# Summing a mixture of experts' outputs on the chip by 0/1 matmuls, in place of a scatter to DRAM and a read back

## The reference, cut to what matters

```python
g_sel = jnp.argmax(lc, axis=-1)
lf_sel = jnp.take_along_axis(lf, g_sel[:, None, None], axis=1)[:, 0]
top_v, top_i = lax.top_k(lf_sel, TOP_K_FINE)
top_w = jax.nn.softmax(top_v, axis=-1)
gates = p_sel * one_hot(g_sel) * fine
h = jax.nn.silu(hg) * hu * gates
y = y + jnp.einsum('tef,efd->td', h, w_down[e])
...
x = x + hier_moe(rmsnorm(x, g2), ...)
return rmsnorm(x, final_norm_g)
```

## Time and profile before

| | |
|---|---|
| median of 3 runs | 735.38 us (735.12 to 735.39) |
| span of the profiled execution | 733.9 us |
| which of the runs was profiled | not given; the median lies 1.5 us above its span |
| TensorE busy | 594.7 us (81%) |
| VectorE / ScalarE / GpSimd busy | 24% / 15% / 12% |
| moved by DMA | 238.7 MB, of them 9.46 MB by gathers and scatters |
| expert stage, first gate/up to end of the last down product | 224.4 to 702.8 us |

### The profile page before, as it was taken

The page is one execution under the profiler, slowest core; times in us unless marked ns, Lnnn a source line. Parts: engine busy times, 40 slices in busy tenths (PEclk is TensorE's granted clock), DMA queues, the critical chain, the costliest instruction groups (busy, mean ns, idle before and its releaser), DMA issues.

```text
span 733.9 us, 8110 instructions
## 1 busy us (share of the span) xinstructions
PE 594.7 (81%) x3112; PEld 316.7 (43%) x3112; DVE 176.2 (24%) x322; ACT 107.1 (15%) x202; POOL 88.0 (12%) x146
## 2 busy tenths in 40 slices
PE   7999999999888999999776776778777777777820
PEld 5999999878753333333222222222222222222200
DVE  5554248514456010101000001000000100000037
ACT  6422342203210000000000000000000000000013
POOL 1000000000022212121121111111211111110000
PEclk9999999999979999999999999999999999999975
DMA  9930600286189999999999999999999999999756
GB/s 290 346 98 3 229 1 1 81 340 269 58 330 342 399 415 415 416 417 415 417 415 416 417 416 417 418 415 416 416 417 416 417 416 415 417 417 418 274 148 227
DMA packets 57128, 238.71 MB, mean 325 GB/s; under 512 B 9382, under 2 KB 16567, under 8 KB 40723
## 3 DMA queue, kind: packets, MB, share of 16 engines
q1 hardware_dynamic: 51987, 228.96, 78.9%
q0 software_dynamic: 5120, 9.46, 3.5%
HBM read 232.48 MB, written 13.24 MB: 335 GB/s over the span
## 4 chain that ended last, share of the span: by engine, by line
SPq 51%; PE 34%; DMA 6%; DVE 4%; issue 3%; ACT 1%; POOLq 0%; POOL 0%; DVEq 0%
SPq L458 33%; SPq L465 18%; PE ps L1283 12%; PE ps L1354 7%; PE ps L1445 5%; DMA w<-in_moe_w_up 3%; PE ps L1465 2%; PE ps L1380 1%; DMA y_rows<-ybuf,idc_y 1%; PE ps L1247 1%; PE ps L1249 1%; PE ps L1248 1%; DMA gain<-in_norm_g 1%; DVE yfin L826 1%; DVE x_sb L826 1%
## 5 line engine op out<-in xcount | busy, mean ns | idle before, releaser
L1445 PE MATMUL ps<-w,xT 128*64 128x512 f32 x1024 | 231.1, 596 | 57.5 <-DMA w<-in_moe_w_up 57.5
L1445 PEld LDWEIGHTS ps<-w,xT 128*64 128x64 f32 x1024 | 72.7, 137 | 214.1 <-issue 151.3
L1465 PE MATMUL ps<-wd,hexT 128*64 128x512 f32 x512 | 118.6, 604 | 27.7 <-DVE hexT L1164 27.7
L820 DVE TENSOR_TENSOR hexp<-silu_g,ps 128x256 f32<-128x256 f32 x32 | 13.5, 422 | 419.7 <-ACT silu_g L795 419.7
L594 POOL DMA_INDIRECT y_rows<-ybuf,idc_y x32 | 32.9, 1029 | 380.0 <-ACT ybuf L799 380.0
L1465 PEld LDWEIGHTS ps<-wd,hexT 128*64 128x64 f32 x512 | 38.1, 138 | 87.4 <-issue 52.8
L795 ACT ACTIVATE silu_g<-ps 128x256 f32<-128x256 f32 x32 | 12.3, 384 | 279.3 <-PE ps L1445 279.3
L1283 PE MATMUL ps<-hT_hi,wi_hi 128*128 128x288 f32 x224 | 48.7, 299 | 0.0
L1283 PE MATMUL ps<-hT_lo,wi_hi 128*128 128x288 f32 x224 | 48.0, 296 | 0.0
L799 ACT COPY ybuf<-ps 128x512 f32<-128x512 f32 x32 | 18.8, 586 | 179.6 <-PE ps L1465 179.6
L582 POOL DMA_INDIRECT xg<-hn_rows,idc_x x32 | 33.8, 1055 | 27.5 <-POOL idc_x L579 27.5
(11 more groups left out here) (194 smaller groups left out, 507.0 us busy)
## 6 DMA issues: line engine op xcount, KB each, us to landing
w<-in_moe_w_gate SPq DMA_DIRECT2D x64, 1024.0 KB, 18.9
w<-in_moe_w_up SPq DMA_DIRECT2D x64, 1024.0 KB, 23.7
wd<-in_moe_w_down SPq DMA_DIRECT2D x64, 1024.0 KB, 22.2
wo<-in_w_out SPq DMA_DIRECT2D x2, 2048.0 KB, 11.0
yfin<-y_rows SPq DMA_DIRECT2D x8, 512.0 KB, 6.0
x_sb<-in_x_prompt SPq DMA_DIRECT2D x4, 512.0 KB, 8.6
hn_rows<-hn2p SPq DMA_DIRECT2D x4, 512.0 KB, 3.0
out<-yfin SPq DMA_DIRECT2D x4, 512.0 KB, 2.6
```

The costliest lines, as they stand in the source:

```text
L1445: last = mm(ps[64 * h:64 * h + 64, 1, :], lhs, w1[s][:, :, k, h * (F // 2):(h + 1) * (F // 2)], start=(k == 0), stop=(k == KD - 1))
L1465: last = mm(ps[64 * h:64 * h + 64, 3, :], lhs, wd[s][:, c, h * 512:(h + 1) * 512], start=(c == 0), stop=(c == F // P - 1))
```

## The change

The scatter, the DRAM tensor `y_rows`, the read back and `yfin` are gone. Each block's down product is scaled by its gate on ScalarE into `y_hi` (rounded to float32r), and VectorE writes the rest of it into `y_lo`. VectorE also builds `home`, a tile of 0 and 1 with one column for each of the 576 tokens: 1 where the block's row belongs to that token and half. TensorE multiplies `home` with `y_hi` and `y_lo` for each of the five token tiles (`send_home`): four one-pass matmuls of 512 columns, two on partitions 0 to 63 into one PSUM bank and two on 64 to 127 into another. VectorE adds the two banks to `x_sb` (`add`, two instructions of 512 columns). The five tiles of block n - 1 are done within block n: three of them inside gate/up, one behind `transpose_x`, one behind `transpose_act`. A pair of banks is free again once the add two tiles back is done.

The routing makes a second table, the gate of each row (`gate_of`), by 20 more small matmuls for the first blocks and 20 for the further ones. All 32 blocks are written out; the check for further blocks stands between blocks 29 and 30 (`LAST` = 30), with all homes and adds of block 29 ahead of it, and block 30 has no homes of an earlier block. The index copies on GpSimd are gone for the 32 blocks.

```diff
-            def scatter(col, s, n, done, i):
-                if not (isinstance(i, int) and i == 0):
-                    pool.wait_ge(y_out[s], 16 * i)
-                nc.gpsimd.tensor_copy(idc_y[:, s:s + 1], idx[:, 1, bass.ds(col, 1)]).then_inc(idc_ready, 1)
-                pool.wait_ge(idc_ready, done)
-                pool.wait_ge(y_ready, n + 1)
-                pool.sem_inc(idc_seen, 1)
-                nc.gpsimd.indirect_dma_start(
-                    out=y_rows, out_offset=bass.IndirectOffsetOnAxis(ap=idc_y[:, s:s + 1], axis=0),
-                    in_=ybuf[:, s, :], in_offset=None,
-                    bounds_check=4 * T - 1, oob_is_err=False).then_inc(y_out[s], 16)
...
+            def high(S, n, done, buf, gate):
+                act.wait_ge(S["dn_ps"], done)
+                nc.scalar.activation(y_hi[:, buf, :], ps[:, 3, :], ACT.Copy, scale=gate).then_inc(S["hi_ready"], 1)
...
+            def low(S, n, buf, row, gate):
+                ts(home[:, buf, :], row_ids[:], row, None, ALU.is_equal)
+                dve.wait_ge(S["hi_ready"], n + 1)
+                stt(y_lo[:, buf, :], ps[:, 3, :], gate, y_hi[:, buf, :].bitcast(F32), ALU.mult,
+                    ALU.subtract).then_inc(S["lo_ready"], 1)
+
+            def add(S, n, j, turn, seen):
+                m = TOK[j]
+                dve.wait_ge(S["home_ps"], seen)
+                for h in range(2):
+                    c = slice(h * (D // 2), (h + 1) * (D // 2))
+                    last = tt(x_sb[0:m, j, c], ps[0:m, 4 + 2 * (turn % 2) + h, :], x_sb[0:m, j, c], ALU.add)
+                last.then_inc(S["added"], 1)
...
+            def turn(n, adds, more=True):
+                if adds:
+                    for j in range(3):
+                        add_first(n - 1, j)
+                work_h(main, n)
                 if more:
-                    work(n + 1)
-                work_hT(n)
...
+                    work(main, n + 1)
+                if adds:
+                    add_first(n - 1, 3)
+                work_hT(main, n)
+                if adds:
+                    add_first(n - 1, 4)
...
+            def send_home(S, buf, j, turn):
+
+                n, t = TOK[j], slice(j * P, j * P + TOK[j])
+                for part, y in enumerate((y_hi, y_lo)):
+                    for h in range(2):
+                        r = slice(64 * h, 64 * h + 64)
+                        last = mm(ps[0:n, 4 + 2 * (turn % 2) + h, :], home[r, buf, t], y[r, buf, :], start=(part == 0),
+                                  stop=(part == 1))
+                last.then_inc(S["home_ps"], 1)
...
+            def turn(n, homes, more=True):
+                s, need = n % NSLOT, 32 * (n // NSLOT + 1)
+
+                def between(k):
+                    if homes and k in (1, 3, 5):
+                        home_first(n - 1, k // 2)
+
+                gate_up(main, n, s, w1_in[s], need, between)
+                if more:
+                    transpose_x(main, (n + 1) % NSLOT, xg_in[(n + 1) % NSLOT], 16 * ((n + 1) // NSLOT + 1))
+                if homes:
+                    home_first(n - 1, 3)
+                transpose_act(main, n)
+                if homes:
+                    home_first(n - 1, 4)
```

More of the change, by code:

```diff
@@ L65 @@
 NSLOT = 3
-PRE = [(NE - s + NSLOT - 1) // NSLOT for s in range(NSLOT)]
-ROUNDS = NE // NSLOT
+SPARE = 2
+LAST = NE - NSLOT + 1
 OUTSIDE = 4096
@@ L236, in build @@
     hexT = post("hexT", [P, 2, P])
+    routing_at = where["end"]
     t_g = post("t_g", [P, NT, NG])
@@ L254, in build @@
     t_k = post("t_k", [P, NT * 2, MAX_J])
+    back = region(routing_at, where["zp"])
+    y_hi = back("y_hi", [P, 2, D // 2], F32R)
+    y_lo = back("y_lo", [P, 2, D // 2], F32R)
+    home = back("home", [P, 2, T], F32R)
     p1 = region(where["zp"], pool_end)
@@ L371, in build, with blocks_past @@
     segs = ((0, 0, HT, 0, 0), (1, 0, SEQ - HT, HT, 0), (1, SEQ - HT, HT, SEQ, 1))
[L375 to L384, removed]
+    def blocks_past(eng, before, body, after):
         eng.wait_ge(nov_ready, 1)
@@ L388, in blocks_past, with nothing @@
         with eng.If(count > 0):
+            before()
             with eng.Fori(0, count) as b:
                 body(b)
-        return count
+            after(count)
+    def nothing(*_):
+        return None
     with nc.Block() as block:
@@ L509, in _ @@
-            with sp.Fori(1, ROUNDS) as i:
-                for s in range(NSLOT):
-                    refill(i, s)
-            for n in range(NSLOT * ROUNDS, NE):
-                refill(n // NSLOT, n % NSLOT)
+            for n in range(NSLOT, NE):
+                s, done = n % NSLOT, n - NSLOT + 1
+                sp.wait_ge(main["half_ps"], done)
+                load_gate_up(n, s, halves=(0,))
+                sp.wait_ge(main["gu_ps"], done)
+                load_gate_up(n, s, halves=(1,))
+                sp.wait_ge(main["dn_ps"], done)
+                load_down(n, s)
@@ L1189, in finish @@
+            blocks_past(dve, before_past, block_past, nothing)
+            work(main, LAST)
+            for n in range(LAST, NE):
+                turn(n, n > LAST, n < NE - 1)
             def finish(j):
@@ L1482, in _ @@
-            experts(pe, lambda i, s: turn(i, s, not (isinstance(i, int) and NSLOT * i + s == NE - 1)))
-            def block_past(b):
-                transpose_x(0, PRE[0] + b + 1)
-                gate_up(NE + b, 0, PRE[0] + b + 1)
-                transpose_act(NE + b)
-                down(NE + b, 0, PRE[0] + b + 1)
-            blocks_past(pe, block_past)
+                last.then_inc(S["dn_ps"], 1)
+            def send_home(S, buf, j, turn):
[6 more added lines that the diff above has]
+                last.then_inc(S["home_ps"], 1)
@@ L1494, with after_past @@
+            def after_past(count):
+                pe.wait_ge(spill["added"], count * NT + 1)
+            blocks_past(pe, before_past, block_past, after_past)
+            transpose_x(main, LAST % NSLOT, xg_in[LAST % NSLOT], 16 * (LAST // NSLOT + 1))
+            for n in range(LAST, NE):
+                turn(n, n > LAST, n < NE - 1)
+            for j in range(NT):
+                home_first(NE - 1, j)
 _INS = ["x_prompt", "x_sample", "state_conv", "state_pool", "norm1_g", "w_in", "conv_w", "pool_w", "pool_scale",
```

394 lines of the change are left out of this document (196 added, 198 removed).

## The result

The changed kernel takes **770.76 us** (769.66 to 771.41) against 735.38: 1.0476 times the time before, interval 1.0463 to 1.049. That is 35.4 us slower, where 12.6 were forecast. Its profiled execution took 769.66 us, with a span of 767.8, 21.2 us above the 746.6 of the forecast's sum; the median misses its 748.0 by 22.8, mainly because the profiled execution was 1.1 us shorter than the median. (Of experiment 5, the kernel without `y_lo`, only one execution counts for the total, because its profiled one ran part of the way at a lower clock.)

What follows compares the result with a forecast made beforehand. PE's chain, 15.52 us a block against a DMA floor of 15.60, was to bound the kernel. 29 blocks (450.1) plus start, block 0, bubble, last blocks and tail (296.5) gave 746.6; 1.5 added, 748.0 us, range 728 to 772.

Steps and rivals of the forecast that it cites:

- rival 3: Homes: every change empties the array and exposes a weight load; home 0.885 us, block 16.26, total 770; chance 0.14.
- PE's chain becomes the bound, not the DMA: Blocks from expert 1 on: PE chain of 15.52 us sets the time; DMA floor 15.60, three experts in hand.
- The fourth add holds hexT; down starts at G+3.24: Add between copies xT and hexT: delays hexT, down product at G+3.24 instead of G+2.05, +1.19 us a block.
- The two others fall where PE waits anyway: Homes behind transpose_x and the transposes of hexp: lie in PE's waiting time, so only three homes add time.
- The halves pair: Home matmuls on partitions 0-63 and 64-127: run side by side, 0.455 us a home.
- I take 0.09 on both sides of each home: 0.64 us: Homes inside gate/up: 0.455 us plus a 0.09 gap each side; three add 1.92 us, gate/up 8.80.
- Its four weight loads fit in: Each home: four weight loads of 0.11 us fit within its 0.455 us.
- Start of expert 0 unmoved at 224.4: Before the blocks: first gather about 1 us earlier, 20 table matmuls give back some 2.2; start left at 224.4.
- Block 0 at 15.5: First block: 12.9 as before, 2.2 for 20 more table matmuls, 0.4 for two VectorE table operations.
- I had priced the clock at nothing within blocks: PE clock: no cost within blocks, PE never idle over about 1.5 us; up to 2 us possible in the bubble.
- Bubble 9.5, block 30 12.4, tail 19.6: End: 9.5 us delay at the check before block 30, block 30 without homes 12.4, tail 19.6 instead of 31.1.
- gather and scatter 0.54 a block: DMA stream: a gather costs 0.54 us a block, scatters the same; removing scatters lowers the floor from 16.14 to 15.60.

Runs made afterwards that it cites:

- experiment 7: The changed kernel without homes and adds for experts 0 to 30, whose outputs are left out of the sums: 717.19 us.
- experiment 1: The changed kernel with the fourth add of a block behind the copy hexT instead of ahead of it: 745.88 us.
- experiment 4: The changed kernel with a home's four matmuls reordered, both parts of one half and then both of the other: 770.88 us.
- experiment 3: The changed kernel with the third expert's down weights issued only when the first gather has landed: 766.74 us.
- experiment 10: The changed kernel with fourth add behind hexT, homes 0 and 1 together, third expert's down weights behind the first gather, and check at the very end: 721.47 us.
- experiment 2: The changed kernel with the first two homes of a block in one place, behind the fourth gate/up step: 760.82 us.

## Why the prediction was wrong

The direction and the bound held; the loss was 35.4 us instead of 12.6, because three terms of the sum were too small: a home inside gate/up (14.1 us in all), the start of expert 0 (3.9) and block 0 (3.2). The time lies within the stated 728 to 772 only because that range was drawn up to rival 3. Rival 3's 770 itself is met in part by luck: its block of 16.26 is 0.23 us longer than the measured 16.03, some 7 us in all, and the start and block 0, which it had no more right than the forecast, make up for these 7.

- **PE's chain becomes the bound, not the DMA**: right. Experiment 7 measures the floor at 15.61 (forecast 15.60), and the changed kernel never waits for weights.
- **The fourth add holds hexT; down starts at G+3.24** (G is the end of gate/up): right, G+3.23 (304.38 to 307.61). But 1.19 is not what the place of the add costs: moving it gives 0.90, as homes 3 and 4 are then no longer hidden (experiment 1). "The two others fall where PE waits anyway" held only because of that wait.
- **The halves pair**: right, in either order (experiment 4).
- **"I take 0.09 on both sides of each home: 0.64 us"** is the step that failed, worth 14.1 of the 21.2 us. The 0.09 was right on both sides. What was missing is that the first weight load behind each change of shape starts only with its matmul: 0.11 us on the way in and 0.06 on the way out, three times a block, 0.51 us; a home measured 0.81 us. "Its four weight loads fit in" is true of the loads of the second step alone. The rule quoted from the Trainium skill (TensorEngine Tiling (Array Packing), Key Properties), that changing the tiling mode drains TensorE, agrees with the two gaps; that the loads stay behind them is what these runs add. I judged it by the gap alone, although the first gate/up had 7.09 us (behind warm-up products over the full array, L1219) and the later ones 7.04 behind a down product of their own shape, which is just such a load. Rival 3 had 0.43 for gaps and load where 0.35 was measured.
- **Start of expert 0 unmoved at 224.4**: wrong by 3.9. I counted the index copies that went, and not that SP's wait hung on them: the semaphore `idc_seen` that SP waits for is still raised, but no longer behind the copies, so the 2 MB of down weights are issued ahead of the first gather (experiment 3). The transfers on SP's queue that stood behind that wait were not followed.
- **Block 0 at 15.5**: wrong by 3.2. The mean granted clock is 0.82 in gate/up of block 0, 0.93 in the table and 0.71 in down, where block 0 of the kernel before had 1.00 throughout, so the products run in part at 1.2 GHz: gate/up takes 8.55 for 7.09, down 5.05 for 3.65, 2.9 us together; the rest is the table, 4.1 us where it was 1.2 and 3.8 were forecast. I had priced the clock at nothing within blocks. The slow gate/up goes with the 2.36 us wait for the gather: without the wait it takes 7.09 (experiments 3 and 10). The slow down product stays without the wait. It stands behind the row of 30 small matmuls, where the kernel before had 10 and kept its clock; whether they are the cause was not tried.
- **Bubble 9.5, block 30 12.4, tail 19.6**: right within 0.3 (the terms given for the bubble add up to 9.35 and those for the tail to 19.5; neither matters). The clock did not fall in the bubble: it was 1.00 there, and gate/up behind it took 7.09. Block 31 was 0.5 too low, by the same exposed loads.
- **Unrolling free, gather and scatter 0.54 a block**: right (0.9999; 0.53).

## What to carry to other kernels

Matmuls of another shape put between those of a tuned product cost, besides their columns, a fixed amount for each place (here 0.35 us): put them together in few places, and count one place as two gaps and two weight loads that nothing hides. An add or a copy that needs a product of the same block must not stand ahead of the one that the next product waits for. And when a small operation is removed, ask what its semaphore had been holding back: here 2 MB of weights that then went ahead of the rows that everything waited for.

## What was not expected of the hardware

- Matmuls on different halves of the rows overtake one another: with hi, lo, hi, lo in the program of experiment 4, both hi start at 300.94 and both lo at 301.28.
- The DMA share stays at 1.00 to 1.02 whether the stream of weights is the bound (416 GB/s before) or has time to spare (402 GB/s in the change), and even the full rate is no sign of a bound: experiment 10 has 415 and 416 GB/s and never waits for weights. What tells them apart are the waits. Whether the stream has time to spare shows in SP's own rows: an issue of 1 MB takes 0.33 to 0.55 us in the change near 510 us and 1.9 to 3.0 in the kernel before, and its data land in 8 to 11 us against 19 to 24.
- With 30 small matmuls for the tables in block 0, the down product behind them ran in part at 1.2 GHz in the change and in each kernel made from it: 5.05 us in the change, 5.29 in experiment 3, 6.46 in experiment 10, at most 6.62 (experiment 2), where 3.65 is its time at 2.4 GHz, whether the first gather had been waited for or not.
